# A hybrid decoder step: causal query blocks of 16, 128, 128, 128, 128 rows in place of 128, 128, 128, 128, 16

## What is computed

```python
def mla_attend(q_lat, q_rope, c_kv, k_rope, q_pos, k_pos):
    s = (jnp.einsum('bqhc,bkc->bhqk', q_lat, c_kv).astype(jnp.float32)
         + jnp.einsum('bqhr,bkr->bhqk', q_rope, k_rope).astype(jnp.float32)) * ATTN_SCALE
    mask = k_pos[None, :] <= q_pos[:, None]
    p = jax.nn.softmax(jnp.where(mask, s, -jnp.inf), axis=-1)
    return jnp.einsum('bqhk,bkc->bqhc', p.astype(c_kv.dtype), c_kv)
```

## Time and profile before

| | us |
|---|---|
| median of 3 runs | 1513.22 (1513.07 to 1514.79) |
| the profiled execution | 1515.17 |
| its span, first to last instruction | 1513.2 |
| PE busy | 1445.9 |
| DVE busy | 689.2 |
| ACT busy | 527.0 |
| POOL busy | 233.8 |
| mean granted PE clock | 0.983 of full |
| the heads, first score to last outputs | 94.7 to 309.3 |

### The profile page before, as it was taken

How to read it: one execution, slowest core, us unless ns; L and a number is a source line. 1 busy time by engine, 2 the same in 40 slices (tenths; PEclk the granted TensorE clock), 3 DMA queues, 4 the chain that set the end, 5 groups by cost and what they waited for, 6 DMA issues and landing times.

```text
span 1513.2 us, 26366 instructions
## 1 busy us (share of the span) xinstructions
PE 1445.9 (96%) x10332; PEld 1310.8 (87%) x10332; DVE 689.2 (46%) x958; ACT 527.0 (35%) x841; POOL 233.8 (15%) x327
## 2 busy tenths in 40 slices
PE   9999999997898999999999999999899999999997
PEld 9756666554688999999999989999799999999996
DVE  4535555532258323222322576887833332233355
ACT  4135454432234322112222247882432211222224
POOL 0020000100056000000000345234620000000034
PEclk9999999998999999999999999999999999999999
DMA  7230000023121333312233222222122331223301
GB/s 203 68 88 19 16 12 22 0 64 103 45 84 57 87 91 98 101 56 84 83 94 115 63 63 63 67 79 88 56 84 83 104 105 55 84 83 94 115 1 59
DMA packets 180547, 111.09 MB, mean 73 GB/s; under 512 B 25608, under 2 KB 178781, under 8 KB 180480
## 3 DMA queue, kind: packets, MB, share of 16 engines
q1 hardware_dynamic: 179888, 109.37, 24.8%
q0 software_dynamic: 592, 0.79, 0.2%
HBM read 107.11 MB, written 3.02 MB: 73 GB/s over the span
## 4 chain that ended last, share of the span: by engine, by line
PE 83%; DVE 8%; ACT 4%; POOL 2%; issue 2%; SPq 1%; DMA 0%; DVEq 0%; ACTq 0%; POOLq 0%
PE ps L495 53%; PE ps L549 6%; PE ps L773 3%; PE ps L720 3%; PE ps L734 3%; DVE xT L1668 2%; PE ps L754 2%; DVE wl L1396 1%; PE ps L688 1%; ACT wh L1080 1%; PE ps L858 1%; PE ps L841 1%; PE ps L885 1%; PE ps L628 1%; DVE xl L1674 1%
## 5 line engine op out<-in xcount | busy, mean ns | idle before, releaser
L495 PE MATMUL ps<-xh,wl 128*128 128x280 f32 x1584 | 334.7, 292 | 0.0
L495 PE MATMUL ps<-xh,wh 128*128 128x280 f32 x1584 | 333.3, 292 | 0.6 <-DVE wl L1396 0.5
L495 PE MATMUL ps<-xl,wh 128*128 128x280 f32 x1584 | 331.7, 291 | 0.0
L495 PEld LDWEIGHTS ps<-xh,wh 128*128 128x128 f32 x1584 | 252.5, 189 | 1.6 <-issue 1.0
L495 PEld LDWEIGHTS ps<-xh,wl 128*128 128x128 f32 x1584 | 252.9, 189 | 0.0
L495 PEld LDWEIGHTS ps<-xl,wh 128*128 128x128 f32 x1584 | 250.3, 188 | 0.0
L1396 DVE TENSOR_TENSOR wl<-raw,wh 128x2048 fp32r<-128x2048 f32 (+2 forms) x79 | 198.0, 2507 | 99.7 <-ACT wh L1080 99.7
L1080 ACT ACTIVATE wh<-raw 128x2048 fp32r<-128x2048 f32 (+2 forms) x79 | 162.9, 2061 | 204.0 <-PE ps L495 190.8
L1714 DVE TENSOR_TENSOR ht<-sg,ps 128x560 f32<-128x560 f32 x44 | 32.5, 738 | 273.1 <-PE ps L495 264.1
L1311 ACT ACTIVATE hh<-ht 128x560 f32 (+1 forms) x44 | 29.6, 672 | 271.6 <-DVE ht L1714 271.6
L1898 POOL TENSOR_TENSOR acc<-xT 128x560 f32<-128x560 f32 x4 | 5.6, 1399 | 726.2 <-DVE xT L1611 669.3
(11 more groups left out here) (306 smaller groups left out, 2373.3 us busy)
## 6 DMA issues: line engine op xcount, KB each, us to landing
raw<-in_ffn_w_gu SPq DMA_DIRECT2D x176, 256.0 KB, 3.6
raw<-in_ffn_w_down SPq DMA_DIRECT2D x48, 384.0 KB, 4.3
raw<-in_lru_w_in SPq DMA_DIRECT2D x16, 512.0 KB, 4.5
Ctok<-in_cache_latent SPq DMA_DIRECT2D x48, 128.0 KB, 2.0
raw<-in_mla_w_o SPq DMA_DIRECT2D x16, 256.0 KB, 3.7
raw<-in_ffn_w_down SPq DMA_DIRECT2D x16, 256.0 KB, 5.1
raw<-in_lru_w_o SPq DMA_DIRECT2D x16, 256.0 KB, 3.3
raw<-in_mla_w_in SPq DMA_DIRECT2D x9, 256.0 KB, 5.4
```

The lines of the kernel that those rows point to most:

```text
L495: mm = pe.matmul(ps[:, 1024 * jp + 512 * h:1024 * jp + 512 * h + TH], w[:, k, col:col + P], x[:, k, h * TH:(h + 1) * TH], start=(k == 0 an ...
```

## The change

The block of 16 queries comes first: the blocks are now the queries 0 to 15, 16 to 143, 144 to 271, 272 to 399 and 400 to 527 (`QB`), with 16, 144, 272, 400 and 528 keys. `SC_AT` says where in PSUM each block's scores lie; the last block starts 16 columns ahead of bank 3, so that its first 16 columns are written into bank 2 by one product and the other 512 into bank 3 by another.

The mask square of 128 columns still lies on the diagonal. A block now ends 16 keys into a 128-key tile, and only its last 16 queries see those keys: `turn` transposes that piece from rows 96 to 127 of `Pr` alone, 32 columns of output, and the other tiles in full. Block 0 is transposed as a full square, with rows that hold zeros or old values; they are never read. Block 4's transposes no longer fit one bank: the fourth and the small one go to bank 5, after a wait for the read of block 3.

`read_pt` takes the full tiles with one activation, and the 16 last queries of the small piece with a second (blocks 1 to 3); block 4 takes three tiles, the fourth tile and the corner with three activations. `pt_rd` counts five times a head, not six. The two `Pr` buffers are cleared whole at the start.

```diff
--- before.py
+++ after.py
@@ -48,6 +48,8 @@
 EARLY = 4
 NEG = -1.0e30
 PR_AT = (0, 128, 384, 768, 1280, 1808)
+QB = tuple((0, META) if i == 0 else (META + P * (i - 1), P) for i in range(5))
+SC_AT = (1024, 1536, 1024, 1536, 2048 - NP)
 XR = T // 5
 UP = 3 + NP
 UL = UP + B * (3 + TS)
@@ -724,40 +726,40 @@
 
             def scores(h, u, i):
 
-                n = P if i < 4 else META
-                bank = 512 * (2 + i % 2)
+                q0, n = QB[i]
+                at, w = SC_AT[i], q0 + n
                 if above_zero(h * 5 + (0, 0, 1, 2, 4)[i]):
                     pe.wait_ge(sc_exp, h * 5 + (0, 0, 1, 2, 4)[i])
-                w = P * i + n
-                q = Q[u][:, P * i:P * i + n]
+                q = Q[u][:, q0:w]
                 if i < 4:
-                    pe.matmul(ps[0:n, bank:bank + w], q, K[u][:, 0:w], start=True, stop=False)
-                    mm = pe.matmul(ps[0:n, bank + P * i:bank + w], identb[:], maskb[:], start=False, stop=True)
+                    pe.matmul(ps[0:n, at:at + w], q, K[u][:, 0:w], start=True, stop=False)
                 else:
-                    pe.matmul(ps[0:n, 1024:1536], q, K[u][:, 0:512], start=True, stop=True)
-                    pe.matmul(ps[0:n, 1536:1536 + n], q, K[u][:, 512:NP], start=True, stop=False)
-                    mm = pe.matmul(ps[0:n, 1536:1536 + n], identb[0:n, 0:n], maskb[0:n, 0:n], start=False, stop=True)
-                mm.then_inc(sc_sum, 1)
+                    pe.matmul(ps[:, at:at + META], q, K[u][:, 0:META], start=True, stop=True)
+                    pe.matmul(ps[:, at + META:at + NP], q, K[u][:, META:NP], start=True, stop=False)
+                pe.matmul(ps[0:n, at + q0:at + w], identb[0:n, 0:n], maskb[0:n, 0:n], start=False, stop=True).then_inc(sc_sum, 1)
 
             def turn(h, u, i):
 
-                n = P if i < 4 else META
+                n = QB[i][1]
                 pe.wait_ge(sc_nrm, h * 5 + (i + 1))
-                if above_zero(h * 6 + max(0, i - 1)):
-                    pe.wait_ge(pt_rd, h * 6 + max(0, i - 1))
+                if above_zero(h * 5 + (0, 0, 1, 2, 3)[i]):
+                    pe.wait_ge(pt_rd, h * 5 + (0, 0, 1, 2, 3)[i])
                 bank = 512 * (4 + i % 2)
-                for j in range(i + 1):
-                    kk = P if j < 4 else META
-
-                    m = P if j == 0 else n
-                    at = PR_AT[i] + j * P
-                    mm = pe.transpose(ps[0:kk, bank + j * n:bank + j * n + m], Pr[u][0:m, at:at + kk],
-                                      ident[0:m, 0:m])
+                for j in range(max(1, i)):
+                    if j == 3:
+                        pe.wait_ge(pt_rd, h * 5 + 4)
+                        bank += 512 - 3 * P
+                    mm = pe.transpose(ps[:, bank + j * P:bank + (j + 1) * P],
+                                      Pr[u][:, PR_AT[i] + j * P:PR_AT[i] + (j + 1) * P], ident[:])
+                if i > 0:
+                    kk = P if i < 4 else META
+                    mm = pe.transpose(ps[0:kk, bank + i * P:bank + i * P + 32],
+                                      Pr[u][96:P, PR_AT[i] + i * P:PR_AT[i] + i * P + kk], ident[96:P, 96:P])
                 mm.then_inc(pt_sum, 1)
 
             def outputs(h, u):
 
-                pe.wait_ge(pt_rd, h * 6 + 6)
+                pe.wait_ge(pt_rd, h * 5 + 5)
                 pe.wait_ge(v_cp, h * 2 + 2)
                 if above_zero(h):
                     pe.wait_ge(o_lo, h)
@@ -1129,22 +1131,27 @@
                                    ACT.Copy).then_inc(s_lte, 1)
 
             def exp(h, u, i):
-                n = P if i < 4 else META
-                w = P * i + n
+                q0, n = QB[i]
+                w = q0 + n
                 act.wait_ge(sc_max, h * 5 + (i + 1))
-                act.activation(Pr[u][0:n, PR_AT[i]:PR_AT[i] + w], ps[0:n, 512 * (2 + i % 2):512 * (2 + i % 2) + w],
+                act.activation(Pr[u][0:n, PR_AT[i]:PR_AT[i] + w], ps[0:n, SC_AT[i]:SC_AT[i] + w],
                                ACT.Exp, bias=mx[0:n, i % 2:i % 2 + 1],
                                accum_out=rsum[0:n, i % 2:i % 2 + 1]).then_inc(sc_exp, 1)
 
             def read_pt(h, i):
-                n = P if i < 4 else META
-                m = min(i + 1, 4)
+                q0, n = QB[i]
+                m = max(1, min(i, 3))
                 bank = 512 * (4 + i % 2)
                 act.wait_ge(pt_sum, h * 5 + (i + 1))
-                act.activation(PT[:, 0:m, P * i:P * i + n],
-                               ps[:, bank:bank + m * n].rearrange("p (j q) -> p j q", j=m), ACT.Copy).then_inc(pt_rd, 1)
+                ins = act.activation(PT[:, 0:m, q0:q0 + n],
+                                     ps[:, bank:bank + m * P].rearrange("p (j q) -> p j q", j=m)[:, :, 0:n], ACT.Copy)
+                if i in (1, 2, 3):
+                    ins = act.activation(PT[:, i, P * i:P * i + META],
+                                         ps[:, bank + P * i + META:bank + P * i + 2 * META], ACT.Copy)
                 if i == 4:
-                    act.activation(PT4[:], ps[0:META, bank + 4 * n:bank + 5 * n], ACT.Copy).then_inc(pt_rd, 1)
+                    act.activation(PT[:, 3, q0:q0 + n], ps[:, bank + 512:bank + 512 + P], ACT.Copy)
+                    ins = act.activation(PT4[:], ps[0:META, bank + 512 + P + META:bank + 512 + P + 2 * META], ACT.Copy)
+                ins.then_inc(pt_rd, 1)
 
             def read_k(p):
                 act.wait_ge(k_sum, p + 1)
@@ -1485,15 +1492,15 @@
                 dve.tensor_copy(V[0:n, kt, h * 512:(h + 1) * 512], ps[0:n, bank:bank + 512]).then_inc(s_vd, 1)
 
             def top_score(h, i):
-                n = P if i < 4 else META
-                w = P * i + n
+                q0, n = QB[i]
+                w = q0 + n
                 dve.wait_ge(sc_sum, h * 5 + (i + 1))
-                dve.tensor_reduce(mx[0:n, i % 2:i % 2 + 1], ps[0:n, 512 * (2 + i % 2):512 * (2 + i % 2) + w], AX.X,
+                dve.tensor_reduce(mx[0:n, i % 2:i % 2 + 1], ps[0:n, SC_AT[i]:SC_AT[i] + w], AX.X,
                                   ALU.max, negate=True).then_inc(sc_max, 1)
 
             def normalise(h, u, i):
-                n = P if i < 4 else META
-                w = P * i + n
+                q0, n = QB[i]
+                w = q0 + n
                 dve.wait_ge(sc_exp, h * 5 + (i + 1))
                 dve.reciprocal(rsum[0:n, 2 + i % 2:3 + i % 2], rsum[0:n, i % 2:i % 2 + 1]).then_inc(sc_inv, 1)
                 dve.wait_ge(sc_inv, h * 5 + (i + 1))
@@ -1543,7 +1550,7 @@
                     read_q(h + 1, v)
 
             for u in range(2):
-                dve.memset(Pr[u][:, PR_AT[4]:PR_AT[5]], 0.0)
+                dve.memset(Pr[u][:], 0.0)
             read_q(0, 0)
             read_k(0)
             for u in range(2):
```

## The result

The changed kernel takes 1521.18 us (median of 5 runs, 1519.68 to 1522.84) against 1513.41 us before: 1.0052 times, 95% interval 1.0037 to 1.0066. It is 7.8 us slower. I had forecast 1.3 us more, or 1514.5 us, and 1519 us was the end of my range. Its profiled execution took 1522.74 us, with a span of 1520.6 us. The instruction counts and the busy times of PE (1447.9 us) are nearly those of before; ACT does 905 instructions instead of 841.

What follows compares the result with a forecast made beforehand. TensorE was taken to bound the heads, busy for 130.55 of 132.80 us. Seven pairs at +0.16 us (+1.1) and first and last heads (+0.2) gave +1.3 us: 1514.5 us on the 1513.22 us median, range 1506.5 to 1519.

Steps and rivals of the forecast that it cites:

- The prices: TensorE unit costs: 0.00085 us a column and record; a small transpose 0.37 us in the place of 0.11.
- turn 1 with score 2 and turn 2: TensorE's transposes and score between, in an even head: 1.49 us against 1.44 us, +0.05.
- The even head: Whole even head on TensorE: +0.15 us, from -0.04 up to the end of score 4 and +0.19 after.
- its front: Start of an even head, block 0's shrunken score and transposes: 0.77 us where 0.72 us stood, +0.05.
- Rival B: Faster: small transposes cost their weight load alone, 0.06 us, pulled ahead under the full one; 1505.8 us; chance 25%.
- The tail: Score 4 to outputs: the maximum, exp, read chain takes 2.37 us against PE's own 2.32; +0.19 us a head.
- rival C: Slower: the last read's three activations don't overlap, 0.21 us more in each of 14 heads; 1517.4 us; chance 26%.
- The front of the odd head: Start of an odd head: DVE's smaller first maximum lets the keys start earlier, taken as 0.10 us saved.
- a pair: An even and an odd head together: 0.16 us more; seven pairs +1.1 us.
- The ends: First and last head: the first shorter by 0.6 us, the last +0.8 us, at least 0.4; together +0.2 us.
- The clearing: Whole clearing of both Pr buffers on DVE at the start: 0.2 us at most, put into the first head's 0.6.
- Rival D: Idle time lowers TensorE's clock: 1.75 us for one more stretch, 1527 us with one a pair; chance 6%.

Runs made afterwards that it cites:

- the run of the full pieces: Changed kernel with the small 32-row transposes taken as full 128-row ones and the reads moved to match: 1512.42 us, 0.9985 of the kernel before.
- the other two mends: Late wait last and clearing early; in the changed kernel with full transposes for small pieces and block 4's read ahead of exp 4: 1503.91 us, 0.9931.

## Why the prediction was wrong

**What held.** The prices. The small transposes cost 0.26 us more each, and turn 1 with score 2 and turn 2 took 1.50 us (175.87 to 177.37) against the 1.49 written. Score 3 lost 0.19 us, turn 3 with the queries behind it took 0.17 us more (0.18 written), and score 4 took 1.14 against 1.17. The even head came out at +0.14 against +0.15, partly by luck: its front was 0.63 us and not 0.77 (less of the exposed loads showed than I had summed), and its tail made up for it. Rival B falls with the run of the full pieces.

The Trainium skill, TensorEngine Tiling, section Key Properties (a change of tiling mode drains the engine), agrees with the 0.10 us that stands ahead of each small transpose in this trace and goes with its form.

**The tail.** The chain itself was right: from the end of score 4 to the end of the read 184.34 - 182.02 = 2.32 us, as summed. The mis-sized term was the last one, 0.05 us from read to outputs. I took it from nothing that showed a late wait with others queued behind it; it measured 0.24 us in even heads and 0.35 in odd ones. The edit that puts the late wait last took 0.10 and 0.21 us of it. So the tail costs 0.38 us (2.56 - 2.18) and 0.48 us, not 0.19. That is rival C's place and its sign (outputs 2.6 us after score 4) but not its mechanism: the three activations do overlap (183.65, 184.02, 184.18).

**The front of the odd head.** I took 0.10 us off because the first maximum shrinks. It gave 0.00: the keys start 1.83 us after the head in both kernels. What ends last there is ACT's high half of the outputs, and DVE's low half behind it: in both kernels the low half starts 0.97 us after the head, 0.16 to 0.17 us after the high half is over. The maximum ended 0.10 us ahead of that start in the kernel before, so making it shorter freed nothing.

These two terms add 0.19 + 0.29 + 0.10 = 0.58 us to a pair. The front of the even head (0.14 us) and small differences in both heads take 0.25 us back. So the pair is +0.49 us instead of +0.16, and seven pairs +3.4 us instead of +1.1.

**The ends.** With the clock kept up in both kernels, the traces confirm the working: from the first score of head 0 to that of head 1 9.79 us against 10.45 us (-0.66, forecast -0.6), and from the first score of head 15 to the last outputs' last record 19.22 us against 18.40 (+0.82, forecast +0.8). Both kernels hold the idle products there, which cost something themselves. Without them and without a stretch head 0 took 9.32 us (waits reordered) against 10.10 (-0.78). The clearing, put at 0.2 us at most and into the first head's 0.6, costs 0.44 us ahead of it.

**The clock.** Rival D, which I gave 6% and looked for in the pairs, decided the rest. With idle products at both ends the two kernels stand 4.0 us apart (1518.17 and 1514.13), of which the pairs are 3.4 us; without them 7.8 us. In the pairs behind head 1 the clock stays at 1.00 in both, as I argued. It is in the first two heads that the changed kernel falls to the lower level: there is no work of a head before to fill PE's waits, and the change takes columns out of just these scores. Widening them again brought the clock back there as well, in the one trace taken. I had seen that idle time brings the clock down, in the earlier trace rows, and asked only whether the new waits would do it, not whether less work in a place already half idle would. By the traces taken the stretch in head 1 is the regular one and that in head 0 comes in some executions; how often was not measured run by run.

The step that failed, then, is the sum for the ends: its chains were right, and it put the clock of the first two heads at nothing. The two stretches there cost 1.46 and 1.69 us where both come, and the idle products at the start gave back 3.1 us of the median. The other is the sum for a pair: the term from read to outputs and the front of the odd head were too small by 0.58 us, and the pairs came out 2.3 us over the forecast.

## What to carry over

Where a chain on another engine becomes the later one, look at what is queued behind the wait that it releases: two waits that were met long before cost 0.10 and 0.21 us while they stood behind the late one, and moving them ahead of it gave that back. Narrower tiles that end in a piece of another form can cost more than the columns they save; the pieces in the common form, one read ahead of an exp and the other two mends together turned +7.8 us into -10.2 us against the kernel before on the same chip. And work taken out of a stretch in which TensorE already waits can be paid back in clock: read the granted clock there before counting it as a gain.

## What I had not expected of the hardware

Adding 66 bf16 products of 128 columns, whose results nobody reads, made the changed kernel 3.1 us faster in the median (1.0025 against 1.0052 of the kernel before, which is 4.0 us). A transpose of 32 rows into 32 columns of output held PE 0.17 us where one of 128 rows into 128 columns held it 0.11 us. Clearing 1808 f32 columns took 1.56 us, 0.00086 us a column, where 528 columns had taken 1.05 / 2 = 0.53 us, 0.00099 a column; I had 1.8 us from the smaller ones.
